# A diffusion trunk's first stage reordered: modulation products ahead of the token transposes, constants split, filler products between pairs

## The reference

```
s_lat = silu(c)[:, None, :];  s_ctx = silu(c_ctx)
for layer in range(2):
    mod = split(s_lat @ mod_w[layer] + mod_b[layer], 6)
    h = modulate(rms_norm(x, norm_mix_pre[layer]), mod[0], mod[1])      # xn * (1 + scale) + shift
    if layer == 0:
        modc = split(s_ctx @ mod_w[layer] + mod_b[layer], 6)
        hc = modulate(rms_norm(ctx, norm_mix_pre[layer]), modc[0], modc[1])
        y, _ = hybrid_mixer(h, hc, hyb_w_in[0], ...)                    # DeltaNet heads + GQA heads
    else:
        y = short_conv_mixer(h, ...)
    x = x + mod[2] * rms_norm(y, norm_mix_post[layer])
    h = modulate(rms_norm(x, norm_ffn_pre[layer]), mod[3], mod[4])
    x = x + mod[5] * rms_norm(conv_ffn(h, ...), norm_ffn_post[layer])
```

## Time and profile before

| | before |
|---|---|
| median of 3 runs | 1841.1 us (1837.04 to 1845.08) |
| profiled execution, its own time | 1844.14 us |
| its span in the profile | 1842.4 us |
| PE busy | 1732.9 us (94%) |
| DVE busy | 979.2 us (53%) |
| ACT busy | 704.0 us (38%) |
| POOL busy | 314.1 us (17%) |

### The profile page before, as it was taken

How to read it: one execution, slowest core, us unless ns; L and a number is a source line. 1 busy time by engine, 2 the same in 40 slices (tenths; PEclk the granted TensorE clock), 3 DMA queues, 4 the chain that set the end, 5 groups by cost and what they waited for, 6 DMA issues and landing times.

```text
span 1842.4 us, 22819 instructions
## 1 busy us (share of the span) xinstructions
PE 1732.9 (94%) x9187; PEld 1456.4 (79%) x9187; DVE 979.2 (53%) x1245; ACT 704.0 (38%) x1056; POOL 314.1 (17%) x220
## 2 busy tenths in 40 slices
PE   6899997989988999989999999998999899999997
PEld 4688887888988956667788888887888788888886
DVE  2633367777787566755644444436446644444222
ACT  2433433444434477733333333223223244443321
POOL 3000014553464344512000000110002000000000
PEclk9899998999999967887999999997999799999999
DMA  9113141212221323032222332321332122232221
GB/s 323 57 54 92 23 149 47 69 47 70 92 69 47 115 91 115 24 92 68 91 92 91 97 105 83 106 89 46 97 110 92 46 92 91 92 108 90 86 91 58
DMA packets 160943, 161.16 MB, mean 87 GB/s; under 512 B 11367, under 2 KB 159192, under 8 KB 160728
## 3 DMA queue, kind: packets, MB, share of 16 engines
q1 hardware_dynamic: 160856, 159.92, 27.3%
HBM read 157.81 MB, written 2.10 MB: 87 GB/s over the span
## 4 chain that ended last, share of the span: by engine, by line
PE 84%; DVE 7%; ACT 4%; issue 2%; POOL 1%; DMA 1%; SPq 0%; DVEq 0%; ACTq 0%; POOLq 0%
PE ps L467 18%; PE ps L468 18%; PE ps L469 18%; PE ps L710 3%; PE ps L689 3%; PE ps L715 3%; ACT mod_raw_c L1083 2%; PE ps L838 2%; PE ps L543 2%; PE ps L801 1%; PE ps L818 1%; PE ps L819 1%; PE ps L775 1%; PE ps L820 1%; DVE w_lo L1365 1%
## 5 line engine op out<-in xcount | busy, mean ns | idle before, releaser
L1365 DVE TENSOR_TENSOR w_lo<-w_raw,w_hi 128x2048 fp32r<-128x2048 f32 x100 | 229.0, 2291 | 510.5 <-ACT w_hi L1045 510.5
L467 PE MATMUL ps<-h_hi,w_hi 128*128 128x512 f32 x968 | 378.3, 391 | 0.4 <-DVE w_lo L1365 0.4
L468 PE MATMUL ps<-h_lo,w_hi 128*128 128x512 f32 x968 | 377.7, 390 | 0.0
L469 PE MATMUL ps<-h_hi,w_lo 128*128 128x512 f32 x968 | 377.5, 390 | 0.0
L1045 ACT ACTIVATE w_hi<-w_raw 128x2048 fp32r<-128x2048 f32 x100 | 191.1, 1913 | 335.4 <-PE ps L469 305.7
L1889 POOL TENSOR_TENSOR mod_raw_c<-mod_raw_c 128x1024 f32<-128x1024 f32 (+2 forms) x120 | 189.2, 1579 | 142.6 <-ACT mod_raw_c L1083 135.7
L467 PEld LDWEIGHTS ps<-h_hi,w_hi 128*128 128x128 f32 x968 | 182.2, 188 | 38.4 <-DVE w_lo L1365 0.8
L469 PEld LDWEIGHTS ps<-h_hi,w_lo 128*128 128x128 f32 x968 | 182.2, 188 | 38.0
L468 PEld LDWEIGHTS ps<-h_lo,w_hi 128*128 128x128 f32 x968 | 182.2, 188 | 37.3
L467 PE MATMUL ps<-mid_hi,w_hi 128*128 128x512 f32 x338 | 133.0, 393 | 0.0
L469 PE MATMUL ps<-mid_hi,w_lo 128*128 128x512 f32 x338 | 131.9, 390 | 0.0
(11 more groups left out here) (326 smaller groups left out, 2764.9 us busy)
## 6 DMA issues: line engine op xcount, KB each, us to landing
w_raw<-in_ffn_w_up SPq DMA_DIRECT2D x44, 1024.0 KB, 5.1
mod_raw_c<-in_mod_w SPq DMA_DIRECT2D x40, 1024.0 KB, 5.2
w_raw<-in_ffn_w_down SPq DMA_DIRECT2D x16, 896.0 KB, 5.0
w_raw<-in_sc_w_in SPq DMA_DIRECT2D x12, 1024.0 KB, 5.2
w_raw<-in_hyb_w_in SPq DMA_DIRECT2D x9, 1024.0 KB, 5.3
mod_raw_a<-in_mod_w SPq DMA_DIRECT2D x8, 1024.0 KB, 12.9
w_raw<-in_ffn_w_down SPq DMA_DIRECT2D x8, 1024.0 KB, 5.3
w_raw<-in_sc_w_out SPq DMA_DIRECT2D x4, 1024.0 KB, 5.3
```

The costliest lines, as they stand in the source:

```text
L467: mm(dst, hi, xh[:, k0 + k, :], start=first and k == 0, stop=False)
L468: mm(dst, hi, xl[:, k0 + k, :], start=False, stop=False)
L469: i = mm(dst, lo, xh[:, k0 + k, :], start=False, stop=last and k == nk - 1)
L1365: V.tensor_tensor(wlo[s][:, :], raw[s][:, :], f32(whi[s][:, :]), ALU.subtract).then_inc(sem("w_lo"), 1)
```

## The change

SP issues only the first two squares of `const` (identity and ones) first. Four pairs go ahead of `cin` and `xin`, four behind. The other 19 squares come behind the first two weight units. Pairs 6 and 7 get a semaphore each.

PE takes pairs 0 to 3 right after the `vrow` transposes, then transposes ctx and x, then takes pairs 4 to 7. Behind each pair stands `fill(3)`: three matmuls of the identity with two squares of constants, 256 columns each, whose result nobody reads (bank 2). `post_stat(0)` moves behind pair 7, `post_stat(1)` behind the turning of `mod_row`. DVE's order follows; in it `split_lo(1)` moves from ahead of `apply_pre(0)` to behind it. ACT waits for four pairs instead of eight ahead of `split_hi`, with `deviation(0)` and `deviation(1)` still ahead of that.

```diff
-            sp.dma_start(const[:, :, :].rearrange("p k n -> p (k n)"), A["const"]).then_inc(sem("const_in"), 16)
+            sp.dma_start(const[:, 0:2, :].rearrange("p k n -> p (k n)"), A["const"][:, 0:2 * P]).then_inc(sem("const_in"), 16)
...
-            sp.dma_start(cin[:, :, :], A["ctx"][0].rearrange("(n p) c -> p n c", p=P)).then_inc(sem("ctx_in"), 16)
-            sp.dma_start(xin[:, :, :], A["x"][0].rearrange("(n p) c -> p n c", p=P)).then_inc(sem("x_in"), 16)
...
             for j in range(8):
+                if j == 4:
+                    sp.dma_start(cin[:, :, :], A["ctx"][0].rearrange("(n p) c -> p n c", p=P)).then_inc(sem("ctx_in"), 16)
+                    sp.dma_start(xin[:, :, :], A["x"][0].rearrange("(n p) c -> p n c", p=P)).then_inc(sem("x_in"), 16)
...
             for u in range(2):
                 sp.dma_start(rv[u][:, :, :], w_in[:, :, u * UW:(u + 1) * UW]).then_inc(sem(f"w_raw{u}"), 16)
+            sp.dma_start(const[:, 2:, :].rearrange("p k n -> p (k n)"), A["const"][:, 2 * P:]).then_inc(sem("const_in"), 16)
```

```diff
+            def fill(n):
+
+                for _ in range(n):
+                    mm(bank(2, UW), ident, const[:, 0:2, :].rearrange("p k n -> p (k n)"), start=True, stop=True)
+
+            def mod_rows(j):
+
+                if j in (0, 2, 4, 6, 7):
+                    pe.wait_ge(sem(MOD_IN[j]), 16 * MOD_IN.count(MOD_IN[j]))
+                if j >= 2:
+                    pe.wait_ge(sem("mrow"), j - 1)
+                for k in range(KC):
+                    i = mm(bank(j % 2, UW)[0:2], cvec[:, k, :], mraw_a[j][:, k, :], start=k == 0, stop=k == KC - 1)
+                i.then_inc(sem("mod_a"), 1)
+
+            pe.wait_ge(sem("cvec"), 2)
+            for j in range(4):
+                mod_rows(j)
+                fill(3)
+            pe.wait_ge(sem("mrow"), 4)
             pe.wait_ge(sem("ctx_in"), 16)
...
+            for j in range(4, 8):
+                mod_rows(j)
+                fill(3)
+            post_stat(0, CTX, 5)
             pe.wait_ge(sem("mrow"), 8)
             for m in range(16):
                 i = tr(bank(7, 2, 2 * m), mod_row[0:2, m * P:(m + 1) * P], const[0:2, C_ID, 0:2])
             i.then_inc(sem("mod_a"), 1)
+            post_stat(1, SEQ, 3)
```

```diff
-            act.wait_ge(sem("mod_a"), 8)
+            act.wait_ge(sem("mod_a"), 4)
...
+            dve.wait_ge(sem("sd"), 2)
+            V.tensor_copy(SXX, bank(6)[:, NL:2 * NL])
+            rstd(1, SEQ)
             split_lo(0, 0)
+            dve.wait_ge(sem("rrow"), 1)
+            apply_pre(0, lambda c: xc[:, c, :], ctmp, bank(5, CTX), CTX, 4, lambda c: modv[:, 0, c, 1:2], hc_hi, hc_lo)
             split_lo(1, 1)
             dve.wait_ge(sem("rrow"), 2)
-            apply_pre(0, lambda c: xc[:, c, :], ctmp, bank(5, CTX), CTX, 4, lambda c: modv[:, 0, c, 1:2], hc_hi, hc_lo)
             apply_pre(1, lambda c: x[:, c, :], tmp, bank(3), SEQ, 0, lambda c: modv[:, 0, c, 0:1], h_hi, h_lo)
```

More of the change, by code:

```diff
@@ L217, in mod_at @@
             return [j for j, q0 in enumerate(MOD_LEVEL) if q0 + lag == q]
+        MOD_IN = ["mod_a0", "mod_a0", "mod_a1", "mod_a1", "mod_a2", "mod_a2", "mod_a3", "mod_a4"]
         def sq_adds(idx):
@@ L369, in _ @@
             for j in range(8):
+                if j == 4:
+                    sp.dma_start(cin[:, :, :], A["ctx"][0].rearrange("(n p) c -> p n c", p=P)).then_inc(sem("ctx_in"), 16)
+                    sp.dma_start(xin[:, :, :], A["x"][0].rearrange("(n p) c -> p n c", p=P)).then_inc(sem("x_in"), 16)
                 src = A["mod_w"][0].rearrange("(k p) n -> p k n", p=P)[:, :, j * UW:(j + 1) * UW]
-                sp.dma_start(mraw_a[j][:, :, :], src).then_inc(sem(f"mod_a{j // 2}"), 16)
+                sp.dma_start(mraw_a[j][:, :, :], src).then_inc(sem(MOD_IN[j]), 16)
             for u in range(2):
                 sp.dma_start(rv[u][:, :, :], w_in[:, :, u * UW:(u + 1) * UW]).then_inc(sem(f"w_raw{u}"), 16)
+            sp.dma_start(const[:, 2:, :].rearrange("p k n -> p (k n)"), A["const"][:, 2 * P:]).then_inc(sem("const_in"), 16)
             sp.dma_start(alog[:, 0:8], A["dn_a_log"][0].rearrange("d h -> (d h)").unsqueeze(0).to_broadcast([P, 8])).then_inc(sem("gate_in"), 16)
@@ L529, in _ @@
             pe.wait_ge(sem("vec"), 1)
-            pe.wait_ge(sem("cvec"), 2)
             pe.wait_ge(sem("xev"), KC)
[L533 to L544, removed]
+            for j in range(4, 8):
+                mod_rows(j)
+                fill(3)
+            post_stat(0, CTX, 5)
             pe.wait_ge(sem("mrow"), 8)
@@ L557, in item_stat @@
                     pe.wait_ge(sem("gcv"), 3)
+                    pe.wait_ge(sem("const_in"), 32)
                 for j in range(items[e][1] // P):
@@ L1392, in _, with mod_copy @@
             i.then_inc(sem("vec"), 1)
+            def mod_copy(j):
+                dve.wait_ge(sem("mod_a"), j + 1)
+                V.tensor_copy(mod_row[0:2, j * UW:(j + 1) * UW], bank(j % 2, UW)[0:2]).then_inc(sem("mrow"), 1)
+            for j in range(4):
+                mod_copy(j)
             for p in range(KC // 2):
@@ L1398, in _ @@
                 V.tensor_copy(x[:, c, :], bank(c % 4)).then_inc(sem("xev"), 1)
[L1399 to L1407, removed]
+            for j in range(4, 8):
+                mod_copy(j)
+            rstd(0, CTX)
             dve.wait_ge(sem("mod_a"), 9)
```

## The result

| | before | after |
|---|---|---|
| median | 1839.93 us (6 runs, 1835.05 to 1845.08) | 1852.45 us (6 runs, 1848.19 to 1858.34) |
| profiled execution | 1844.14 us | 1852.42 us |
| span | 1842.4 us | 1850.6 us |

The ratio is 1.0067, with a 95% interval of 1.0046 to 1.0088: 12.3 us slower, between 8.5 and 16.2. The forecast said 13.7 us, and 1854.8 us for the median. The interval holds both the forecast and the first rival's 11.8 us, so the time alone does not choose between them; the traces do.

A forecast was written before the change was run, and what follows sets the result against it. PE was taken as the bound, working pairs without pause before a serial DVE and ACT tail. Last pair +6.5, tail +5.3, one clock loss +1.9 give +13.7 us: 1854.8 against the 1841.1 median; range 1848.5 to 1860.5.

The forecast's parts named there:

- first rival: No further loss of PE's clock beyond pair 0: +11.8 us, 1852.9 us; chance 0.30.
- Start of pair 0: In the prologue, pairs 0 and 1, loaded ahead of x and context, let PE start at 15.9 against 24.94.
- Low clock in pair 0: Pairs begin on an idle PE: about four us at 1.2 GHz, half of it lost, +1.9 us.
- Fills: Behind each pair on PE, three filler matmuls take 1.3 us, hidden by nothing.
- Transposes: Between pairs 3 and 4, DVE's twelve copies bound them: 9.0 us plus 0.25 to pair 4; bounds 8.3 and 11.5.
- Tail: Behind the last pair: context's first chunk after 9.7 us (+3.0), x's first chunk after 19.5 (+5.3).
- Clock: One more fall of PE's clock, likeliest in the transposes or unit 0 on x: +1.9 us.
- Sum: Last pair and tail add 11.8 us, with one further clock loss 13.7 us.
- second thought: In the prologue, without fills and cold clock, four pairs plus transposes end at 39.0, against 38.9 before without statistics.
- cheap fills: A fill takes 0.6 us, eight save 5.6: +6.2 to +8 us, about 1848; chance 0.09.
- products at the low level: Pairs run at the low clock now and fills lift them: -6.2 us, 1834.9; zero at 2.0 us a pair; chance 0.03.

The follow-up runs named there:

- experiment 5: The changed kernel with one filler matmul behind each pair instead of three; ratio to the kernel before 1.0021 (1.0004 to 1.0038).
- Experiment 2: The kernel before with three filler matmuls behind each of the eight pairs, nothing else changed; ratio to the kernel before 1.0072, 13.2 us slower.
- experiment 1: The changed kernel without its 24 filler matmuls; ratio to the kernel before 1.0018 (0.9999 to 1.0036), 3.3 us.
- Experiment 3: The changed kernel with ACT's two weight splits ahead of its two square roots; ratio to the kernel before 1.0062 (1.0041 to 1.0083).
- experiment 9: The kernel of 8 with x's square root, reciprocal and rows moved inside the context's stage; median 1830.04 us, ratio to the kernel before 0.9962.
- experiment 7: The changed kernel without fills, a semaphore per pair, transposes between pairs, tail work under the pairs; ratio to the kernel before 0.9961, 7.2 us faster.
- 8: Experiment 7's kernel with x's square root behind ACT's context chunks, DVE's unit-1 split behind the last mod_row copy; ratio to the kernel before 0.9968.

## Why the prediction was right, point by point

- **Start of pair 0**: 15.9 forecast, 15.47 measured. The stream had begun 0.23 us earlier (the first pair was issued at 7.19, the context's load before at 7.42).
- **Low clock in pair 0**: +1.9 forecast; the pair took 5.37 us against 3.54, +1.8. In other executions it took up to 6.57, so the hit is in part luck.
- **Fills**: 1.3 forecast, 1.49 measured, 1.5 us more over eight. What was left out is the fixed 0.20 us (experiment 5). Experiment 2 shows that they lie wholly on the path, and experiment 1 that they bring back 0.8 us at most, in one sum of the tail.
- **Transposes**: 9.25 us forecast to pair 4, 8.1 measured (37.45 to 45.54), below the lower bound of 8.3. From 40 to 44 DVE had no gaps. This and the early start offset the dearer fills, and the last pair ended at 64.26 where 64.0 was forecast; that it came so near is luck, of errors of about a microsecond each way.
- **Tail**: context 9.7 us behind the last pair forecast, 9.57 measured; x 19.5 and 19.37. Experiment 3 shows the square root's part, 1.5 us.
- **Clock**: one further loss was forecast, of two likely places. It was unit 0 on x, not the transposes, and it cost 1.2 us instead of 1.9. The eight matmul steps from 87.42 to 90.84 took 3.4 us where they take 1.8 at the full clock, so PE lost 1.6; it made up 0.4, as I read it because, being behind, it no longer waited for DVE's chunks (the unit that PE began late in experiment 9 took 10.98 us, against 11.30). The rule of the Trainium skill (TensorE: Matmul & The Clock Gate, Part 4: PE-mode transpose), by which the full clock does not engage for transposes, was given an even chance. This trace does not agree with it: the granted clock is 1.00 through eight us of transposes and, since that column reads 1.00 in the slow pair 0 too, more to the point, pair 4 took 3.61 us.
- **Sum**: 13.7 forecast, 13.05 at the last matmul of unit 0 on x, 12.3 (8.5 to 16.2) in the ratio. X's first chunk moved by 11.86 where the sum without the last clock loss said 11.8 (its tail term is 19.5 less 14.3, which is 5.2 and not 5.3). The forecast's second thought, that starting pairs early brings nothing since the transposes come onto the path, is experiment 1: 1.0018, with x's first chunk 1.4 us later than before.
- **Rivals**: cheap fills and products at the low level both fall, by the fill's 1.49 us and by pairs of 3.54 us. The latter rival's turning point was misworked: with its own terms the sum is zero at about 2.4 us a pair, not 2.0, which changes nothing at 3.54.

## What to carry to other kernels

Filler work to keep a clock up can bring back no more than the low clock costs. Here that was 1.8 us at the start, which it did not prevent, as it came behind, and 0.8 in the tail, which it did, against 11.9 spent on an engine that was the bound already. Moving work to an earlier start gains nothing if what lay beside it moves onto the path: interleave the two (a pair, then two groups of transposes, 1.0 us of PE each), and look for engines that idle under the long stretch before adding anything to it (two weight splits moved, 4.4 us gained in the prologue). In an in-order program, ask of each square root or small sum what stands behind it.

## What the runs showed of the hardware that I had not expected

POOL's adds of 128 x 512 took 1.39 us each in the changed kernel (seven in 9.73 us). Where DVE's weight splits ran beside them, two took 4.26 us with one split (experiment 7) and 6.13 or 6.50 with two (8 and 9). ACT's split is not what slows them: in experiment 3 it ran beside the same seven, and they took 9.74. The undisturbed ones, from the timeline of the changed kernel:

```profile
46.34 9.73 POOL L1904 TENSOR_TENSOR tmp<-tmp,tmp 128x512 f32<-128x512 f32 x7
```

DVE's split took 2.27 to 2.64 us beside them and 2.26 to 2.29 alone. That fits what the Trainium skill says (SBUF — State Buffer, SBUF: two separate sides), that one port pair is shared by the two engines and held for a whole instruction; the stretch was seen, its cause was not tested apart. In experiment 7 it stood behind the 1.5 us that the context's first chunk waited. In 8 and 9 DVE's two small `pre_w` instructions took 1.08 us instead of 0.24 and ended just behind POOL's add.

The clock of PE rose at another moment after pair 0 began in each execution: that pair took 5.37 to 6.57 us in the versions with fills first, and the first three pairs 13.37, 12.84 and 11.87 us in experiments 7 to 9, where three at the full clock would take about 10.6 (an estimate: 48 records 0.2175 us apart, and the last one's 0.38). So one execution's prologue carries one to one and a half microseconds of chance, and the stretch up to the first output projection up to seven.
